# Two-model layer stack on one core: a new first norm, three substitution batches instead of two, softplus sums in float32, and a projection begun one pair sooner

## What is computed

```python
h = rms_norm(x, pre_mix_norm)
proj = h @ w_in                        # q, k, v, z for 8 heads, beta/decay columns, SSD columns
lmat = jnp.where(strict, a_in, 0.0) + jnp.eye(CHUNK)        # one 64x64 per chunk and head
sol = lax.linalg.triangular_solve(lmat, rhs, left_side=True, lower=True, unit_diagonal=True)
...
log_fail = jnp.where(visible, jax.nn.log_sigmoid(-z), 0.0)  # stick-breaking attention
cum_rev = lax.cumsum(log_fail, axis=3, reverse=True)
weights = jnp.where(visible, jnp.exp(jax.nn.log_sigmoid(z) + later), 0.0)
```

## Time and profile before

| | us |
|---|---|
| median of 3 runs | 2231.47 (2230.43 to 2233.69) |
| profiled execution, its own time | 2233.14 |
| its span | 2231.3 |
| TensorE busy | 2142.6 (96%) |
| VectorE / ScalarE / GpSimd busy | 1203.0 / 908.8 / 381.5 |
| mean granted TensorE clock | 0.97 of full |

### The profile page before, as it was taken

The page is one execution under the profiler, slowest core; times in us unless marked ns, Lnnn a source line. Parts: engine busy times, 40 slices in busy tenths (PEclk is TensorE's granted clock), DMA queues, the critical chain, the costliest instruction groups (busy, mean ns, idle before and its releaser), DMA issues.

```text
span 2231.3 us, 26717 instructions
## 1 busy us (share of the span) xinstructions
PE 2142.6 (96%) x9746; PEld 1717.4 (77%) x9746; DVE 1203.0 (54%) x1578; ACT 908.8 (41%) x1283; POOL 381.5 (17%) x322
## 2 busy tenths in 40 slices
PE   7996999999989999998998999999999979999999
PEld 4875888878867888886676888888878848888887
DVE  3695735766366666226564566653354445666522
ACT  4873445344244444224464444432242244444311
POOL 2221121201112222000412122210000022222200
PEclk8998999999999999999998999999999979999999
DMA  6323321121222323221111233232212112333321
GB/s 199 109 63 86 79 82 62 57 76 57 95 66 87 101 95 112 94 87 57 57 47 47 88 101 95 94 112 101 86 62 93 60 35 86 97 101 94 119 91 64
DMA packets 80105, 189.33 MB, mean 85 GB/s; under 512 B 18448, under 2 KB 38928, under 8 KB 80016
## 3 DMA queue, kind: packets, MB, share of 16 engines
q1 hardware_dynamic: 80016, 188.12, 26.6%
HBM read 178.66 MB, written 9.44 MB: 84 GB/s over the span
## 4 chain that ended last, share of the span: by engine, by line
PE 88%; DVE 6%; ACT 3%; DMA 1%; issue 1%; POOL 1%; SPq 0%; DVEq 0%; ACTq 0%
PE acc L245 22%; PE acc L247 22%; PE acc L246 22%; PE acc L2498 1%; PE acc L2500 1%; PE acc L2499 1%; PE bank L1629 1%; PE bank L1908 1%; PE bank L1161 1%; DVE l_tmp L1559 1%; DVE small L1562 1%; PE bank L221 1%; PE bank L223 1%; PE bank L222 1%; PE bank L245 1%
## 5 line engine op out<-in xcount | busy, mean ns | idle before, releaser
L245 PE MATMUL acc<-HH,whi 128*128 128x512 f32 x1624 | 657.9, 405 | 18.3 <-POOL HL L371 7.2
L247 PE MATMUL acc<-HH,wlo 128*128 128x512 f32 x1624 | 638.7, 393 | 0.0
L246 PE MATMUL acc<-HL,whi 128*128 128x512 f32 x1624 | 637.8, 393 | 0.0
L188 DVE TENSOR_TENSOR wlo<-raw,whi 128x1024 fp32r<-128x1024 f32 (+1 forms) x296 | 404.2, 1367 | 309.0 <-ACT whi L182 309.0
L182 ACT ACTIVATE whi<-raw 128x1024 fp32r<-128x1024 f32 (+1 forms) x296 | 327.3, 1107 | 586.3 <-PE acc L247 556.1
L245 PEld LDWEIGHTS acc<-HH,whi 128*128 128x128 f32 x1624 | 308.3, 190 | 89.3 <-DVE wlo L188 14.7
L247 PEld LDWEIGHTS acc<-HH,wlo 128*128 128x128 f32 x1624 | 307.9, 190 | 66.1
L246 PEld LDWEIGHTS acc<-HL,whi 128*128 128x128 f32 x1624 | 308.8, 190 | 62.9 <-issue 4.1
L245 PE MATMUL acc<-FH,whi 128*128 128x512 f32 x528 | 209.0, 396 | 0.0
L247 PE MATMUL acc<-FH,wlo 128*128 128x512 f32 x528 | 208.6, 395 | 0.0
L246 PE MATMUL acc<-FL,whi 128*128 128x512 f32 x528 | 208.6, 395 | 0.0
(11 more groups left out here) (375 smaller groups left out, 2718.2 us busy)
## 6 DMA issues: line engine op xcount, KB each, us to landing
raw<-w SPq DMA_DIRECT2D x258, 512.0 KB, 3.6
raw<-w SPq DMA_DIRECT2D x48, 704.0 KB, 4.0
X<-x SPq DMA_DIRECT2D x4, 512.0 KB, 7.5
x_dram<-small SPq DMA_DIRECT2D x8, 256.0 KB, 4.5
xt_dram<-small SPq DMA_DIRECT2D x8, 256.0 KB, 3.7
a_dram<-l_am SPq DMA_DIRECT2D x8, 256.0 KB, 3.6
l_xt<-xt_dram SPq DMA_DIRECT2D x8, 256.0 KB, 2.9
l_x<-x_dram SPq DMA_DIRECT2D x8, 256.0 KB, 3.8
```

The lines of the kernel that those rows point to most:

```text
L188: nc.vector.tensor_tensor(lo[:, 0:kt * P], raw[u % RAW][:, 0:kt * P], hi[:, 0:kt * P].bitcast(F32), ALU.subtract).then_inc(w_lo_ready, 1)
L245: nc.tensor.matmul(a[:, :], wh, tile(hi, k), start=start and k == 0, stop=False)
L246: nc.tensor.matmul(a[:, :], wh, tile(lo, k), start=False, stop=False)
L247: last = nc.tensor.matmul(a[:, :], wl, tile(hi, k), start=False, stop=stop and k == kt - 1)
```

## The change

Five edits come together.

1. The norm: SP loads `X` first and only a small piece of `cst` and `par`; the rest of both, a 32 x 32 identity at four places (`fold`) and the 32 useful columns of unit 0 (`tab_w`) are loaded behind the fourth weight unit. DVE adds the squares, and one matmul by ones sums them. All 8 scaled tiles have a buffer (`normed_x`); DVE forms `HL` in place of POOL. `begin_pe` multiplies q and k of head 0 together, tile by tile; unit 0 is replaced by eight float32 matmuls of 32 columns each into four quarters of one PSUM bank, added up by four matmuls with `fold`. In the first pass of `prep_pe` unit 4 is multiplied whole, ahead of the sums.
2. Substitution in three batches, heads 0 to 2, 3 to 5, 6 and 7, with new cuts for the DVE pieces and a new order of `spread`, `load_xt` and `load_x` on SP.
3. In `chunks` of the state-space part, part 3 of the filler unit (and part 2 for the second group) moves ahead in the first chunk.
4. `PARTED` keeps only the blocks with key block 2; the others go through `sums` as one float32 matmul. Four of six POOL copies and four of six `low` fall away in each pair.
5. Parts 0 and 1 of `begin(0, ...)` move from the last pair to the end of the pair before.

```diff
+        def norm_dve(dve, c, gain):
+            for k in range(1, KD):
+                dve.wait_ge(sq_ready, c["sq"] + k + 1)
...
+                nc.vector.tensor_tensor(hn[0][:, :], hn[0][:, :], sq[k % 2][:, :], ALU.add).then_inc(sq_added, 1)
+            split_lo(dve, 0, None, 0, KD, early[0])
+            dve.wait_ge(params_in, 32)
+            dve.wait_ge(rms_ready, c["rms"] + 1)
+            for k in range(KD + 1):
+                if k < KD:
+                    nc.vector.scalar_tensor_tensor(out=tile(normed_x, k), in0=tile(X, k), scalar=col(gain[0], gain[1] + k),
+                                                   in1=rs[:, :], op0=ALU.mult, op1=ALU.mult).then_inc(hn_ready, 1)
+                if k:
+                    dve.wait_ge(hh_ready, c["hh"] + k)
+                    nc.vector.tensor_tensor(tile(HL, k - 1), tile(normed_x, k - 1), tile(HH, k - 1).bitcast(F32),
+                                            ALU.subtract).then_inc(h_ready, 1)
+                if k == 1:
+                    split_lo(dve, 1, None, 0, KD, early[1])
...
-        PARTED = [b for b in BLOCKS if b[1] < 3]
+        PARTED = [b for b in BLOCKS if b[1] == 2]
...
+                if i == NP - 2:
+                    begin(0, 0)
+                    begin(0, 1)
...
+        def begin_pe(pe, c):
+            for k in range(KD):
+                pe.wait_ge(h_ready, c["h"] - KD + k + 1)
+                if k == KD - 1:
+                    pe.wait_ge(params_in, ALL_PARAMS)
+                    for j in range(KD):
+                        g = j % 4
+                        last = nc.tensor.matmul(bank[5][NARROW * g:NARROW * (g + 1), :], tab_w[:, NARROW * j:NARROW * (j + 1)],
+                                                tile(normed_x, j), start=j < 4, stop=j >= 4, skip_group_check=True)
+                    last.then_inc(a_pe, 1)
...
-        FIRST_BATCH = 4
+        BATCHES = ((0, 1, 2), (3, 4, 5), (6, 7))
+        BATCH_AT = (0, 64, 0)
...
-        INVERSE_A = {(5, 1): (0, 4), (6, 0): (4, 8), (6, 1): (8, 12), (7, 0): (12, 15), (7, 1): (15, 19), (8, 0): (19, 31)}
+        INVERSE_A = {(4, 1): (0, 0, 4), (5, 0): (0, 4, 8), (5, 1): (0, 8, 11), (6, 0): (0, 11, 14), (6, 1): (0, 14, 17),
+                     (7, 0): (0, 17, 20), (7, 1): (0, 20, 25), (8, 0): (0, 25, 31), (8, 1): (1, 0, 2)}
...
-        INVERSE_B = {0: ((3, 7), (7, 11), (11, 15)), 1: ((15, 18), (18, 22), (22, 26)), 2: ((26, 31),)}
+        INVERSE_B = {0: ((1, 11, 15), (1, 15, 19), (1, 19, 22)), 1: ((1, 22, 26), (1, 26, 31), (2, 0, 5)),
+                     2: ((2, 5, 8), (2, 8, 12), (2, 12, 15)), 3: ((2, 15, 18), (2, 18, 22), (2, 22, 25)),
+                     4: ((2, 25, 31), None, None)}
...
                 if n in range(24, 37, 2):
                     h = (n - 24) // 2
+                    if h == 2:
+                        spread(1, (3,))
+                        load_xt(3)
+                    if h == 5:
+                        spread(2, (6, 7))
+                        load_xt(6)
+                    if h == 6:
+                        load_xt(7)
                     load_x(h + 1)
                     if h == 2:
-                        spread(1)
-                        load_xt(4)
-                    if h + 3 < NH and h != 1:
-                        load_xt(h + 3)
+                        spread(1, (4, 5))
+                    if h in (2, 3):
+                        load_xt(h + 2)
```

More of the change, by code:

```diff
@@ L152, in program @@
         out_stored = sem("out_stored")
+        NORM_COLUMNS, ALL_PARAMS = 9, 16 * 9
+        assert cols.start["eps"] == 0 and cols.start["g_pre_mix"] == 1
         def log_exp(act):
@@ L179, in split_hi @@
             act.wait_ge(raw_in[u % RAW], at(16 * (u // RAW + 1), i, 16 * per // RAW))
-            if u >= SPLIT and first is None:
+            if u >= behind and first is None:
                 act.wait_ge(unit_done, at(u - behind + 1, i, per))
@@ L249, in multiply @@
                 last.then_inc(unit_done, 1)
[L252 to L257, removed]
         def rms_act(act, summed, r, width):
@@ L264, in rms_act, with norm_pe @@
             nc.scalar.activation(rs[:, :], ln[:, :], ACT.Exp, scale=-0.5).then_inc(rms_ready, 1)
[L266 to L270, removed]
-        def norm_act(act, c, made):
[L273 to L276, removed]
+        def norm_pe(pe, c):
+            pe.wait_ge(params_in, 32)
+            pe.wait_ge(sq_added, c["add"] + KD - 1)
+            nc.tensor.matmul(ss[:, :], ones, hn[0][:, :], start=True, stop=True).then_inc(sq_summed, 1)
@@ new lines, in program @@
+        NARROW = 32
+        early = [tuple(place(f"early_{n}{j}", KD * P, FREE + (24 + 4 * j + 2 * m) * TILE, F32R)
+                       for m, n in enumerate(("hi", "lo"))) for j in range(2)]
+        tab_w = place("tab_w", KD * NARROW, FREE + 17 * TILE)
+        normed_x = place("normed_x", KD * S, FREE + 40 * TILE)
+        fold = place("fold", NARROW, FREE + 16 * TILE)
+        def norm_act(act, c, made):
+            for k in range(KD):
+                act.wait_ge(*made(k))
+                square(act, c, tile(X, k), k, sq, hn[0])
+            split_hi(act, 0, None, 0, KD, early[0])
+            act.wait_ge(params_in, 32)
+            rms_act(act, c["ssum"] + 1, c["rms"], D)
+            split_hi(act, 1, None, 0, KD, early[1])
@@ L277, in norm_act @@
             for k in range(KD):
                 act.wait_ge(hn_ready, c["hn"] + k + 1)
-                nc.scalar.activation(tile(HH, k), hn[k % 2][:, :], ACT.Copy).then_inc(hh_ready, 1)
-            split_hi(act, 1, None, 0, KD)
-        def scaled_dve(dve, c, src, gain, used, u0):
-            dve.wait_ge(rms_ready, c["rms"] + 1)
[L285 to L290, removed]
+                nc.scalar.activation(tile(HH, k), tile(normed_x, k), ACT.Copy).then_inc(hh_ready, 1)
@@ L1244, in sb_pe @@
                 if last:
-                    for part in range(3):
-                        begin(0, part)
+                    begin(0, 2)
                 if i:
@@ L1653, in prep_pe @@
                 if p == 0:
+                    chunk_sums_pe(pe)
+                    unit(2 + 2 * h)
                     pe.wait_ge(a_steps, 8)
@@ L1823, in heads_dve @@
             vb(0)
+            inverse_dve(dve, 1, 2, 7)
             xt(0, 5)
@@ L1826, in heads_dve @@
             xt(0, 6)
-            inverse_dve(dve, 1, 0, 3)
+            inverse_dve(dve, 1, 7, 11)
             for h in range(NH):
@@ L2030, in load_l1, with block_rows @@
         def load_l1(sp, c):
-            place_of = [0] + [4 * h + j for h in range(NH) for j in (1, 2)] + [3, 4, 7] + [
+            place_of = [4 * h + j for h in range(NH) for j in (1, 2)] + [3, 4, 7] + [
                 4 * h + j for k in range(NH - 2) for h, j in ((k + 1, 4), (k + 2, 3))] + [4 * (NH - 1) + 4] + list(range(33, 53))
+            def block_rows(h):
+                batch = next(b for b in range(3) if h in BATCHES[b])
+                first = BATCH_AT[batch] + 16 * BATCHES[batch].index(h)
+                return slice(first, first + 16)
             def store_a(h):
@@ L2085, in load_l1 @@
                     load_xt(2)
-                    for h in range(FIRST_BATCH, NH - 1):
-                        store_a(h)
+                    store_a(NH - 2)
                 if n == 24:
```

171 lines of the change are left out of this document (98 added, 73 removed).

## The result

The changed kernel takes 2207.76 us in the median of 4 runs (2202.72 to 2210.1), the kernel before 2230.95 on the same chip (2229.72 to 2233.69). The ratio is 0.990, with a 95% interval of 0.9887 to 0.9913: faster by 1.0%, or 23.2 us. The profiled executions have spans of 2205.8 and 2231.3 us, 25.5 apart, where the prediction's sum was 29.0.

A forecast was written before the change was run, and what follows sets the result against it. TensorE, busy 96% of the span, was taken as the bound, with its waits and half clock to win. From 2233.1, -16.4 - 2.8 - 10.4 + 0.7 + 0.8 + 1.3 - 2.7 + 0.5 = -29.0 gives 2204.1, by the median 2202.5; range 2188 to 2213.

The forecast's parts named there:

- narrow matmuls one after the other: Rival, head: the eight narrow matmuls run serially, not side by side; +5 us, 2207; chance 0.08.
- stage sb in full: Rival, stage sb: the clock falls before the last scores although the gap is short; +7 us, 2210; chance 0.12.
- Head, -16.4 predicted: Start to the first pair's products: their end moves from 65.35 to 49.0 us; bounds -11 and -19.
- The parameters came in time: Rival, head: parameters come late and k = 7 waits for them; 2236 if they come at 62 us; chance 0.02.
- First batch, -2.8: First substitution batch: new cuts reduce DVE's excess from 12.1 to 9.3 us; bounds 0 and -14.
- Second batch, -10.4 and +0.7: First head: 8.8 us wait for `l_small` goes, with 1.6 of half clock; POOL's masks slow nine steps, +0.7.
- Heads 3 and 6, +0.8 and +1.3: SP late: head 3 waits 3.3 us, head 4's 2.5 wait goes, net +0.8; head 6 costs +1.3.
- a delay by DVE in heads 1 to 4: Sign of a wrong prediction: third batch's DVE steps there delay TensorE; they were costed at nothing.
- State-space part, -2.7: Two quarter units of 1.36 us each move into waits at the two starts and are hidden; -2.7 us.
- Stage sb, +0.5: Float32 sums +7.9, filled wait -2.7, half clock avoided -6.4, missing filler in last pair +1.7; bounds -3 and +8.
- the waits only move: Rival, batches: DVE stays over by 12.1; heads 3 and 6 wait 3 us more each; +12, 2214; chance 0.16.
- The clock stays up: Rival: no half clock behind the batch, head 3 or second state-space start; 12 us less, 2190; chance 0.20.

The follow-up runs named there:

- Experiment 6: Changed kernel with needless matmuls in the head, four ahead of the sum of squares and five behind it: 2204.08 us.
- experiment 5: Changed kernel with all eight narrow matmuls accumulated into one quarter of the PSUM bank: 2213.44 us.
- Experiment 7: Changed kernel with batches of four, two and two heads, and the third batch spread one weight load sooner: 2204.22 us.
- Experiment 2: Kernel before with only the three substitution batches and their SP order added: 2222.61 us, ratio 0.997.
- experiment 9: Changed kernel with the third batch's spread and head 6's `l_xt` one weight load sooner, three needless matmuls in head 3's wait: 2201.02 us, ratio 0.988.
- experiment 1: Changed kernel with only the new head; batches, state-space part and stage sb as in the kernel before: 2218.27 us, ratio 0.994.
- experiment 10: Changed kernel with the state-space part's projection quarters put back in their old places: 2207.0 us, ratio 0.9906.
- Experiment 3: Changed kernel with the softplus sums back in fp32r hi/lo pairs: 2202.3 us, ratio 0.9862.
- 8: Changed kernel with needless float32 matmuls in two waits for `HL` and the wait before stage sb's first scores: 2202.31 us, ratio 0.986.

## Why the prediction was right, and where it was off

The direction, the mechanisms and the range (2188 to 2213) held; the time was 5.3 us over the 2202.5 forecast. The time alone would not have told the forecast from two of its rivals, narrow matmuls one after the other (2207) and stage sb in full (2210); the rows did, with 1.92 us for the narrow ones and full clock through the last scores. In its own steps:

- **Head, -16.4 predicted, -13.4 measured: the step that failed.** `X` was forecast to be there at 7.8 and the sum to be done at 10.8; they came at 9.0 and 13.4. I had let `X` flow alone, at 416 GB/s from its first byte. The kernel after, DMA from 0 to 20 us in slices of 0.5, and ACT's last squares:

```profile
GB/s 0 0 0 106 197 303 385 418 401 369 352 385 401 418 377 341 370 421 410 426 401 434 426 410 418 418 418 406 446 415 420 413 248 306 374 356 172 57 147 90
```

```profile
9.02 1.29 ACT L331 ACTIVATE sq<-X 128x512 f32<-128x512 f32 x2 [0.30 <-DMA X<-x]
```

```profile
0.00:9.00 9.00, 0.00 (x0) 0.00 (x0) 2.86 (x5) 4.95 (x7) 1.16 (x5) 1.00 0.82 291
```

  The flow takes 2 us to rise, and `X` is there 1.2 late. By 9.0 us it had moved 2.6 MB (9.0 us at a mean of 291 GB/s, last row), 0.5 MB more than `X`: the small pieces and the first weights, issued behind `X`, shared the way with its last part. How the 1.2 divides between the two is open. And I priced the sum matmul at 0.86, the full clock, where TensorE had stood idle and it took 2.05. Experiment 6 shows that second part. The first `HL` was ready at 17.06 and not 14.7. From there to the end of k = 6 I had 13.2 and it took 12.5; half clock held for 5.7 us, for the 6 of the prediction. The narrow matmuls are exactly the 1.9 chosen, and experiment 5 shows the bound of 6.9 to be right too. From the end of k = 7 to the end of the first pair's products it took 19.0 for 17.8: fold, chunk sums and products each some tenths longer than the rows I took. The parameters came in time; the narrow matmuls did not wait for them.
- **First batch, -2.8:** -3.0 by the leads. Experiment 7 shows how steep this is: with four heads it costs 6.3, with waits for `l_z` and `l_small` that the smaller batch does not have.
- **Second batch, -10.4 and +0.7:** -10.0; the wait fell from 8.84 to 0.39. Experiment 2 shows that the batches alone do it.
- **Heads 3 and 6, +0.8 and +1.3:** +0.1 and +2.4. Waits of 3.53 and 1.50 where 3.3 and 1.3 stood in the argument. That SP's place in its queue sets head 6 is shown by experiment 9, which removed the wait by moving SP's instructions. Between the output sums of heads 3 and 4 TensorE lost another 0.7 (21.70 for 21.03), with a wait of 0.4 for `l_small` in it, just behind the last copy of the third batch on DVE. Experiments 7 and 9, which end that batch in the same place, have the same 0.7. This period is 21.70 in experiment 2 and 21.02 in experiment 1, so the 0.7 come with the three batches. The substitution in the heads was therefore not quite free, though I had costed it at nothing, and a delay by DVE in heads 1 to 4 was one of the prediction's signs of being wrong; it is 0.7 us. That the copy is what delays `l_small` is argued, not tested.
- **State-space part, -2.7:** -3.0, and 2.8 in experiment 10.
- **Stage sb, +0.5:** +0.1, and its four terms one by one: From the second `values` to the third it is 28.32 before and 20.83 after, 7.5 less in spite of 1.96 for float32, so 9.4 for the wait and the clock: the wait 3.3 (2.7), half clock 6.1 (6.4). The float32 sums themselves are 4 x 1.96 = 7.8 longer (7.9). From the third to the fourth it is 11.58 and 13.86: 1.96 and 0.3 for the missing filler (1.7), since DVE, rid of `low`, was hardly late. Here two terms of the sum overlapped: the 7.9 took DVE's `low` as work that ran beside TensorE in all pairs, and the 1.7 reckoned with a chain that still held it. Experiment 3 gives the net price of float32, 5.0. Besides, the clock behind the first scores, which wait 2.98 in both kernels, stood at half for 13.7 us where it was 10.2 before: from there to the first `values` 38.35 and 41.68, so 1.4 beyond the 1.96.

The rival "the waits only move" (2214) was wrong: the first batch gave back 3.0 us, and the waits at heads 3 and 6 were 0.2 longer than forecast and not 3. "The clock stays up" (2190) was wrong for the changed kernel at head 3 and at the state-space part's second start, right behind the first batch (1.00 from 166.9 to 175.0), and describes what experiments 6, 8 and 9 then made of it.

## What to carry to other kernels

Price a wait of the bounding engine as the wait and the work behind it at half clock, but only where that engine sets the pace afterwards: in stage sb 2.7 us of moved work brought 7 us, at the two projections behind the post stages 4.3 us of filling brought nothing. Cheaper precision steps off the bound engine (casts, remainders) are no reason to move their cost onto it: float32 sums cost 5 us here, and 7.8 by their own durations, since in the last pairs the casts and remainders would have cost TensorE a wait. And take several changes apart before keeping them; here one of five cost time, and its cost was hidden by the others.

## What was not expected of the hardware

- **The same wait has different prices.** At the second start of the state-space part nine kernels have the same two waits (1.3, and 1.78 or 1.79). From that `yd` to the next it takes 13.7 us in five of them, 12.05 in one and 10.4 in three. The clock stood at 0.52 for up to 6.8 us, or not at all:

```profile
469.40:483.20 13.80, 13.78 (x64) 11.52 (x64) 6.90 (x11) 2.14 (x3) 5.23 (x4) 0.75 0.09 23
```

```profile
464.60:475.10 10.50, 10.42 (x63) 8.74 (x64) 7.23 (x12) 2.14 (x3) 5.49 (x4) 1.00 0.06 9
```

  The first row is of the changed kernel, the second of experiment 9's, each from one `yd` to the next. Even head 3's wait of 3.46 was followed by full clock in experiment 6, and the same 3.46 in experiment 5 by half clock (24.81 and 27.43 us for the period). So two executions of one kernel differ by several us: those of the changed kernel run from 2202.7 at a mean clock of 0.984 to 2210.1 at 0.981. A step of 3 us in one trace needs its place before it is anyone's merit. What decides between the cases stays open.
- **Four 32-column matmuls side by side** take the time of one, 1.92 us for eight of 512 columns in float32. Going into them and out of them costs at most 0.1 us each: their neighbours start 0.32 and 0.35 apart, where 0.23 is usual.
